# A hybrid layer (state scan, latent attention, expert mixer): the order of TensorE's front, rewritten

## The chip, the cores and the metric
One core of a Trainium2 chip runs the whole layer in one program. The metric is the device time of one execution in microseconds. The five engines are TensorE (PE), VectorE (DVE), ScalarE (ACT), GpSimd (POOL) and SyncE (SP, which only issues DMAs here).

## The reference, cut to what matters
Two groups of 128 tokens, a prompt (g = 0) and a sample (g = 1), go through the same layer of width 1024, all in float32.

```python
def trunk_layer(x, cvec, p, rope=None, ctx=None):
    sh1, sc1, g1, sh2, sc2, g2 = modulation(cvec, p['w_mod'], p['b_mod'])   # 1024 -> 6 x 1024
    h = modulate(x, p['norm1'], sh1, sc1)                                   # rmsnorm * (1 + scale) + shift
    u, c_q, c_kv, k_rope = jnp.split(h @ p['w_in'], IN_SPLITS, axis=-1)
    ssm_out, ssm_state = s5_mixer(u, p, ...)      # diagonal state scan, both directions, gated
    ...                                           # latent attention, 8 heads; the sample also reads 128 cached tokens
    mix = jnp.concatenate([ssm_out, attn], axis=-1) @ p['w_out']
    x = x + g1 * mix
    h2 = modulate(x, p['norm2'], sh2, sc2)
    x = x + g2 * peer(h2, p['w_query'], p['sub_keys'], p['u_table'], p['v_table'])
```

`peer` makes 8 heads of two queries from h2 and scores them against 128 keys each. It takes the 16 best of each, then the 16 best sums, so 128 experts ("picks") per token. It reads a row of u and a row of v for each, and adds gelu(h2 . u) * gate * v. Both groups together take 256 picks for each of 128 partitions. One pick is a gather of 128 rows of 2048 floats (u and v side by side), 1 MB.

## The kernel before
**Stages.** TensorE's order is written out by hand (lines 757 to 897). First come eight steps of the first modulation quarter (`quad_step(0, k)`) and the transposes of the normed inputs; then the S5 scan in four chunks of units u = 0 to 3. Each chunk has `input_weights`, `input_projection`, `input_chunked` and `s5_in` on TensorE; `s5_products`, `s5_scans` and `s5_turns` on DVE; `s5_sums`, `s5_turns` and `s5_last` on POOL; and then `y_local`, `y_carried` and `y_spread` on TensorE again. Between these stand the projections to the latents of both groups, their transposes, the attention of the prompt, and the steps of the second modulation quarter. Then come the gate, the output product of the prompt (`out_projection`), the second norm (`norm2_of`, on rows), its transposes, the queries and scores, and the sample's attention up to its scores.

**The carried state.** `y_carried(u)` (line 582) multiplies four parts of the turned state for each of eight tiles and halves: 64 products, in pairs with the same weights. Chunk 3 uses chunk 0's work area again, so its sums wait for `y_ready` and `last_ready`.

**The loop of picks.** It has 64 iterations `it` of four picks. POOL gathers a pick (line 1316) into one of the memory pages of 8 KB per partition that are in turn. `row_plan` (line 68) fixes which: four at the start (13, 14, 8, 9), 15 from pick 4, 0 and 1 from picks 5 and 6, then 6 and 7 from 24, 3 and 4 from 88. A page is used again when its last pick is accumulated (`row_free`), and a new one when `available` says so. DVE takes the dot product with h2 (line 1626). ACT makes gelu and weight and writes them as a diagonal matrix (`weigh`, line 1061): it waits for all four dots of the iteration, then four small weights, then four diagonals. TensorE adds diagonal times v (`accumulate`, line 746), eight products of 512 columns, and frees the page. In the first 26 iterations TensorE does other work ahead of each accumulation (lines 849 to 896): at `it` 0 the rest of the sample's attention and its whole output product, then rows of the norm, and whole sets of queries and scores. DVE finds the picks of a unit of 32 (`find`, `number`, `normalise`) between its dots; the first unit is split by heads, and the gathers start when `number(0, (0, 1))` is done.

**What sets the order.** Each engine runs its list in order and waits on semaphores. A PSUM bank is given by `bank_plan` (line 84): each name has a bank and a turn, and TensorE's `start` waits until the turn before is emptied. SP loads weights in the order of `PAGES` (line 55) and waits, in that order, until a page's last user is done.

## Time and profile before
| | us |
|---|---|
| median of 3 runs | 973.76 (971.82 to 975.36) |
| profiled execution, its own time | 973.73 |
| its span, first to last instruction | 971.9 |
| TensorE busy in it | 771.5 (79%) |
| DVE busy | 555.8 (57%) |
| POOL busy | 350.2 (36%) |
| ACT busy | 253.8 (26%) |
| bytes moved | 324.21 MB, mean 334 GB/s |

The busy shares are means over stages that have different limits. The view of slices and the view of stretches show how a stage runs; the view in order of time shows who starts when, and the idle time in brackets behind a row is that of the engine just before it, with what ended it. One call of a 512-column product appears as two instructions, so eight products are "x16".

### The profile page before, as it was taken

Reading aid. Unit: us, or ns where it says so; the run is one execution under the profiler, and the core shown is the slowest. Engines: PE = TensorE matmul, PEld = TensorE weight load, DVE = VectorE, ACT = ScalarE, POOL = GpSimd, SP = SyncE. Lnnn points to the kernel's source line nnn. Section 1 sums busy time; section 2 is a strip of 40 time slices with the busy share of each in tenths; the row PEclk is TensorE's granted clock in tenths of the full one; section 3 lists DMA queues with packets and bytes.
Section 4 is the critical chain, followed back from the end, with each engine's and each line's share of the span. In section 5 each row is a group of like instructions: output and inputs, shape, how many; then the busy total and the mean of one; then the engine's idle time right before and its main releaser. Section 6 shows DMA issues by size and latency. Waiting matters only on the chain. (4 is left out here: it accounts for less than half of the span.)

```text
span 971.9 us, 11540 instructions
## 1 busy us (share of the span) xinstructions
PE 771.5 (79%) x4265; PEld 409.0 (42%) x4265; DVE 555.8 (57%) x1211; ACT 253.8 (26%) x804; POOL 350.2 (36%) x326
## 2 busy tenths in 40 slices
PE   3898979884878799989979887886975868677785
PEld 0586655544535355646523333332332323233332
DVE  7923261135742863684476559549847845954543
ACT  3411342123321232232222132213211312222120
POOL 1511341001113434324434543543753544264430
PEclk9899999998789999999989998988999898899898
DMA  9840571722466999999999999999999999999991
GB/s 371 322 162 3 223 321 71 277 98 78 161 259 232 363 420 420 420 395 383 384 421 422 421 419 422 420 420 422 419 420 421 392 423 421 371 417 422 422 421 61
DMA packets 46383, 324.21 MB, mean 334 GB/s; under 512 B 5420, under 2 KB 5996, under 8 KB 8184
## 3 DMA queue, kind: packets, MB, share of 16 engines
q0 software_dynamic: 36864, 268.45, 67.6%
q1 hardware_dynamic: 9096, 54.86, 14.2%
q8 instruction: 33, 0.54, 0.2%
q10 hardware_dynamic: 368, 0.18, 0.1%
q14 instruction: 22, 0.18, 0.0%
HBM read 322.24 MB, written 1.23 MB: 333 GB/s over the span
## 5 line engine op out<-in xcount | busy, mean ns | idle before, releaser
L746 PE MATMUL psum<-mem 128*128 128x512 f32 x1024 | 484.1, 630 | 125.0 <-ACT mem L1077 121.5
L1316 POOL DMA_INDIRECT mem<-uv_table,small x256 | 299.1, 1168 | 434.3 <-PE psum L746 350.5
L1626 DVE CUSTOM_DVE_ANT_0 mem<-mem,h 128x1024 f32<-128x1024 f32 x256 | 309.5, 1227 | 250.9 <-DMA mem<-uv_table,small 248.8
L746 PEld LDWEIGHTS psum<-mem 128*128 128x128 f32 x1024 | 201.7, 202 | 397.7 <-issue 243.7
L1065 ACT ACTIVATE small<-small 128x4 f32<-128x4 f32 x64 | 13.2, 206 | 487.3 <-DVE small L1626 487.3
L1077 ACT ACTIVATE mem<-consts,small 128x128 f32<-128x128 f32 x256 | 80.8, 387 | 0.0
L725 PE MATMUL psum<-hT,mem 128*128 128x128 f32 x512 | 60.2, 280 | 4.8 <-DVE mem L1521 3.3
L725 PEld LDWEIGHTS psum<-hT,mem 128*128 128x128 f32 x512 | 59.9, 196 | 8.6 <-issue 7.0
L1070 ACT ACTIVATE small<-small 128x1 f32<-128x1 f32 x256 | 54.5, 283 | 5.9
L1245 POOL TENSOR_SCALAR small<-small 128x1 f32<-128x1 f32 (+1 forms) x9 | 2.8, 309 | 120.7 <-DVE small L1526 41.7
L462 PE MATMUL psum<-mem,scol 128*32 128x512 f32 x128 | 21.5, 766 | 16.9 <-DMA mem<-w_mod 16.4
L1462 DVE TENSOR_TENSOR mem<-psum,mem 128x512 f32<-128x512 f32 x16 | 9.9, 684 | 42.2 <-PE psum L566 42.2
L1487 DVE SCALAR_TENSOR_TENSOR yb<-h,consts,psum 128x256 f32<-128x256 f32 x4 | 1.9, 481 | 48.1 <-PE psum L602 48.1
L910 ACT COPY late<-psum 128x512 f32<-128x512 f32 (+2 forms) x36 | 19.8, 580 | 35.1 <-PE psum L734 9.6
L707 PE MATMUL psum<-mem,hT 128*128 128x512 f32 x64 | 28.0, 593 | 0.0
L486 PE MATMUL psum<-modrow,consts 128*128 128x512 f32 (+1 forms) x32 | 18.1, 695 | 5.7 <-DVE mem L1512 5.7
L1582 DVE FIND_INDEX8 mem<-mem 128x8 uint32<-128x128 f32 (+1 forms) x64 | 21.8, 352 | 0.0
L1285 POOL TENSOR_TENSOR mem<-mem 128x528 f32<-128x528 f32 x8 | 11.0, 1384 | 29.7 <-DVE mem L1479 28.6
L1626 DVE DVE_READ_ACCUMULATOR2_ANT small<- 128x1 f32 x256 | 21.1, 82 | 0.0
L1579 DVE MAX8 mem<-mem 128x8 f32<-128x128 f32 (+1 forms) x64 | 19.4, 350 | 0.9
L1579 DVE MAX8 mem<-late 128x8 f32<-128x128 f32 x32 | 7.1, 281 | 20.3 <-ACTq L1054 20.3
L707 PEld LDWEIGHTS psum<-mem,hT 128*128 128x128 f32 x64 | 12.1, 190 | 14.8 <-issue 14.8
(193 smaller groups left out, 648.0 us busy)
## 6 DMA issues: line engine op xcount, KB each, us to landing
mem<-w_mod SPq DMA_DIRECT2D x24, 1024.0 KB, 10.4
mem<-w_query SPq DMA_DIRECT2D x8, 1024.0 KB, 9.2
mem<-w_out SPq DMA_DIRECT2D x4, 1024.0 KB, 12.4
mem<-uv_table,small POOLq DMA_INDIRECT x256, 14.6
mem<-w_uq SPq DMA_DIRECT2D x4, 576.0 KB, 5.2
mem<-w_in_u SPq DMA_DIRECT2D x2, 1024.0 KB, 15.6
mem<-w_ukv SPq DMA_DIRECT2D x2, 1024.0 KB, 5.3
mem<-w_in_qkv SPq DMA_DIRECT2D x2, 1008.0 KB, 10.0
```

What stands on the lines that cost most here:

```text
L462: mm = pe.matmul(out[32 * j:32 * j + 32, :], scol[:, k, :], w[:, j, :], start=k == 0, stop=False, tile_position=(0, 32 * j))
L486: mm = pe.matmul(out, ident[lo:hi, j + g:j + g + 1].to_broadcast([hi - lo, P]), modrow[lo:hi, n // 4, :], start=True, stop=True, tile_posi ...
L707: mm = pe.matmul(out, mixT[:, k, P * g:P * g + P], weight(f"out{half}.{k // 4}", 512, 4)[:, k % 4, :], start=first and i == 0, stop=last a ...
L725: mm = pe.matmul(out[:, P * i:P * i + P], weight(m, 512, 4)[:, k % 4, P * i:P * i + P], hT[:, k, P * g:P * g + P], start=k == 0, stop=k == ...
L746: mm = pe.matmul(bank(f"acc_{g}_{half}"), diag[:, pick % DEEP, :], row_of(pick)[:, D + 512 * half:D + 512 * half + 512], start=first and k ...
L910: empties(act.copy(dst, src), name)
L1070: act.activation(wts[:, slot:slot + 1], gel[:, slot:slot + 1], ACT.Copy, scale=gate[:, pick:pick + 1]).then_inc(wts_ready, 1)
L1077: act.activation(diag[:, slot, :], ident, ACT.Copy, scale=wts[:, slot:slot + 1]).then_inc(diag_ready, 1)
L1316: pool.indirect_dma_start(row_of(pick), None, uv_table, bass.IndirectOffsetOnAxis(ap=idx[:, pick:pick + 1], axis=0)).then_inc(row_landed[R ...
L1579: last = dve.max(out_v[:, r, first_:first_ + 8], row)
L1582: last = dve.max_index(out_i[:, r, first_:first_ + 8], out_v[:, r, first_:first_ + 8], row)
L1626: dve.tensor_tensor_reduce(out=row[:, 0:D], in0=row[:, 0:D], in1=h[:, it // NB, :], scale=1.0, scalar=0.0, op0=ALU.mult, op1=ALU.add, accu ...
```

## The change
- TensorE's front has a new order. All four `s5_in` come before the latents. Two steps of modulation quarter 1 at a time are put between the chunks. The sample's query and key projections (`attention_queries(1)`, `attention_keys(1)`) stand behind the prompt's output product, between the first queries and scores. Their weights stay in their pages from the prompt's use, so that three loads (uq2.0, uq2.1, ukv2) are gone.
- Each chunk has its own work area. POOL adds the two parts of the turned state (`sum_ready`), and `y_carried` has half the products.
- The biases of a modulation quarter are added after step 5 and not after step 7. x is loaded after two weight steps and cmat later.
- The second norm for the queries is no longer made on rows and transposed. TensorE multiplies x with a diagonal of the root (`normed_turned`), which transposes and scales at once; scale and shift are columns (`columns_turned`, `norm_columns`), applied in the eviction. The row form of h2, which the dots need, is still made, for the sample only at `it` 22 and 23.
- Queries and scores of the first unit are split in halves (`first_queries`, `first_scores`); the other queries are made in two iterations each. Half of the sample's output product comes before its attention scores, the other half at `it` 4 and 5.
- `weigh` goes pick by pick.
- The pages in turn are other ones and open at other times (`row_plan`, `available`).

```diff
-SCORED = [0, 1, 4, 5, 2, 6, 3, 7]
+SCORED = [0, 0, 1, 2, 4, 5, 3, 6, 7]
+FOUND = [2, 4, 6, 7, 8, 9, 10, 11]
...
-    free, arriving = [13, 14, 8, 9], {4: 15, 5: 0, 6: 1, 24: 6, 25: 7, 88: 3, 89: 4}
+    free, arriving = [6, 7, 8, 9], {4: 4, 5: 13, 16: 15, 64: 0, 65: 1, 96: 2, 97: 3, 120: 5}
...
-            for k in range(4):
+            for k in range(2):
                 load(f"mod0.{k}")
             sp.dma_start(x[:, 0, :], x_prompt).then_inc(x_in, 16)
             sp.dma_start(x[:, 1, :], x_sample).then_inc(x_in, 16)
...
             def y_carried(u):
-                pe.wait_ge(qd_ready, 2 * u + 2)
-                pe.wait_ge(qp_ready, 2 * u + 2)
+                pe.wait_ge(sum_ready, 2 * u + 2)
...
-                        for k, (r, b) in enumerate(((0, 0), (0, 2), (1, 1), (1, 3))):
+                        for r in range(2):
...
+            def normed_turned(g):
+                pe.wait_ge(rootd_ready, g + 1)
                 for q in range(2):
+                    out = start(f"h2T_{g}_{q}")
+                    for i in range(4):
+                        k = 4 * q + i
+                        mm = pe.matmul(out[:, P * i:P * i + P], x[:, g, P * k:P * k + P], root_diag[g], start=True, stop=True)
+                    finish(mm, f"h2T_{g}_{q}")
...
             pe.wait_ge(ssm_ready, 1)
             for half in range(2):
                 out_projection(0, half, range(4), last=True)
+            columns_turned()
...
-            attention_queries(1)
-            attention_keys(1)
-            h2_transposed(0)
-            queries(0, 0)
-            scores(0, 0)
+            attention_queries(1, (0,))
+            normed_turned(0)
+            attention_queries(1, (1,))
+            first_queries(0)
+            attention_keys(1, 0, "k")
+            first_scores(0)
+            first_queries(1)
+            attention_keys(1, 0, "v")
+            first_scores(1)
+            attention_keys(1, 1)
             heads_turned(1)
+            pe.wait_ge(ssm_ready, 2)
+            for half in range(2):
+                out_projection(1, half, range(4), first=True)
             attention_scores(1)
 
             for it in range(NU):
-                if it == 0:
+                if it in (0, 1):
+                    queries(0, 1, it)
+                elif it == 2:
+                    scores(0, 1)
                     probs_turned(1)
+                elif it == 3:
                     attended(1)
                     spread_row("g1", 1)
+                elif it in (4, 5):
                     wait_emptied(pe, "at1")
-                    pe.wait_ge(ssm_ready, 2)
-                    for half in range(2):
-                        out_projection(1, half, range(8), first=True, last=True)
+                    out_projection(1, it - 4, range(4, 8), last=True)
...
             def weigh(it):
...
+                for pick in range(BATCH * it, BATCH * it + BATCH):
+                    slot = pick % DEEP
+                    cut_ = slice(slot, slot + 1)
+                    act.wait_ge(dots_ready, pick + 1)
+                    act.activation(gel[:, cut_], dots[:, cut_], ACT.Gelu_apprx_tanh).then_inc(gel_ready, 1)
+                    act.wait_ge(gates_ready, it + 1)
+                    act.wait_ge(gel_ready, pick + 1)
+                    act.activation(wts[:, cut_], gel[:, cut_], ACT.Copy, scale=gate[:, pick:pick + 1]).then_inc(wts_ready, 1)
                     act.wait_ge(wts_ready, pick + 1)
                     if pick >= DEEP:
                         act.wait_ge(row_free, pick - DEEP + 1)
+                    act.activation(diag[:, slot, :], ident, ACT.Copy, scale=wts[:, cut_]).then_inc(diag_ready, 1)
...
+                for r in range(2):
+                    pool.wait_ge(qp_ready, 2 * u + 2)
+                    pool.tensor_tensor(view(u, r), view(u, r), view(u, 2 + r), ALU.add).then_inc(sum_ready, 1)
...
             def available(page_):
-                if page_ in (13, 14):
-                    pool.wait_ge(y_ready, NC)
-                    pool.wait_ge(last_ready, 2 * NC)
+                if page_ == 6:
+                    wait_filled(pool, "q_1_1")
+                elif page_ == 7:
+                    wait_filled(pool, "v2")
                 elif page_ in (8, 9):
                     pool.wait_ge(h2_ready, 1)
+                elif page_ == 4:
+                    pool.wait_ge(out_used, 1)
+                elif page_ == 13:
+                    pool.wait_ge(out_used, 2)
                 elif page_ == 15:
                     wait_filled(pool, "at1")
                 elif page_ in (0, 1):
-                    wait_filled(pool, f"mix_1_0")
+                    wait_filled(pool, "qry_1_1")
...
             for u in range(NC):
-                if u == 0:
-                    inverse_root(rstd_a[:, 0:2], ms_a[:, 0:2], [(0, 1, QR), (1, 2, KVR)], sqa_ready, 2, rstda_ready)
                 if u + 1 < NC:
                     s5_sums(u + 1)
...
+                if u == 3:
+                    inverse_root(rstd_a[:, 0:2], ms_a[:, 0:2], [(0, 1, QR), (1, 2, KVR)], sqa_ready, 2, rstda_ready)
                 s5_turns(u)
```

The new front on TensorE, from the first `s5_in` on: s5_in(0); chunk and projection pairs; s5_in(1); two steps of quarter 1; s5_in(2); kernels; s5_in(3); latents(0); steps 2, 3; toeplitz; latents_turned(0); y(0); steps 4, 5; latents(1); the prompt's queries and keys; y(1); steps 6, 7; latents_turned(1); heads_turned(0); y(2); attention_scores(0); y(3) carried; two steps of quarter 2; y_spread(3); probs_turned(0); g1 row; attended(0); the gate products between the halves of the output product; two steps of quarter 2; the rest of the output product; columns_turned; rows for the norm.

## Rows read from the trace of the kernel before
**Rows 1.** The page's 40 slices: GB/s that the DMA engines moved in each.
```profile
GB/s 371 322 162 3 223 321 71 277 98 78 161 259 232 363 420 420 420 395 383 384 421 422 421 419 422 420 420 422 419 420 421 392 423 421 371 417 422 422 421 61
```

**Rows 2.** DMA queues: packets, MB, share of 16 engines; the gathers' queue.
```profile
q0 software_dynamic: 36864, 268.45, 67.6%
```

**Rows 3.** TensorE in order of time: start, us, line, operation, count, [idle before].
```profile
40.89 7.14 PE L512 MATMUL psum<-hT,mem 128*128 128x256 f32 x32 [1.93 <-ACT hT L922]
...
115.58 3.90 PE L592 MATMUL psum<-mem 64*64 64x64 f32 x128
...
205.89 7.10 PE L644 MATMUL psum<-mem,yb 128*128 128x512 f32 x16 [2.65 <-DVE h L1536]
212.83 1.04 PE L493 MATMUL psum<-consts,h 128*128 128x128 f32 x8
215.30 7.38 PE L725 MATMUL psum<-hT,mem 128*128 128x128 f32 x64 [1.43 <-ACT hT L910]
223.41 1.16 PE L734 MATMUL psum<-mem,yb 128*128 128x128 f32 x8 [0.73 <-ACT yb L910]
...
228.57 3.69 PE L668 MATMUL psum<-late 96*128 96x256 f32 x16 [1.37 <-ACT late L910]
245.88 3.67 PE L493 MATMUL psum<-consts,mem 128*128 128x128 f32 x16 [13.62 <-DVE mem L1680]
...
256.46 13.90 PE L707 MATMUL psum<-mem,hT 128*128 128x512 f32 x32
270.19 7.03 PE L746 MATMUL psum<-mem 128*128 128x512 f32 x16
...
954.34 8.83 PE L746 MATMUL psum<-mem 128*128 128x512 f32 x16 [2.78 <-ACT mem L1077]
```

**Rows 4.** Stretches: busy us of PE, PEld, DVE, ACT, POOL; clock, DMA, GB/s.
```profile
236.00:340.00 104.00, 78.52 (x267) 43.91 (x268) 58.20 (x155) 25.27 (x77) 29.02 (x31) 0.84 0.68 255
340.00:480.00 140.00, 130.74 (x609) 83.58 (x608) 81.45 (x180) 38.88 (x126) 53.02 (x48) 0.99 0.99 403
...
560.00:946.00 386.00, 294.20 (x616) 122.74 (x617) 252.82 (x573) 98.73 (x362) 181.66 (x151) 0.92 1.01 416
```

**Rows 5.** GpSimd in order of time: first, eighth and thirty-first gather.
```profile
235.47 1.22 POOL L1316 DMA_INDIRECT mem<-uv_table,small  x1 [32.47 <-DVEq L1609]
...
272.35 0.94 POOL L1316 DMA_INDIRECT mem<-uv_table,small  x1 [6.40 <-PE psum L746]
...
349.36 0.94 POOL L1316 DMA_INDIRECT mem<-uv_table,small  x1 [0.78 <-PE psum L746]
```

**Rows 6.** DVE in order of time: first find, first numbers, first and last product.
```profile
225.34 0.49 DVE L1579 MAX8 mem<-late 128x8 f32<-128x128 f32 x2 [17.45 <-ACTq L1054]
...
234.93 0.17 DVE L1607 SCALAR_TENSOR_TENSOR small<-mem 128x16 uint32<-128x16 f32 x1
...
245.74 1.22 DVE L1626 CUSTOM_DVE_ANT_0 mem<-mem,h 128x1024 f32<-128x1024 f32 x1
...
951.58 1.23 DVE L1626 CUSTOM_DVE_ANT_0 mem<-mem,h 128x1024 f32<-128x1024 f32 x1 [1.22 <-DMA mem<-uv_table,small]
```

**Rows 7.** TensorE's waits from 139 to 225 us: in total, times, longest.
```profile
PE psum L493 <- issue: 5.6, 1, 5.6
...
PE psum L697 <- ACT yb L1153: 2.3, 1, 2.3
...
PE psum L474 <- DMA mem<-w_mod: 1.4, 1, 1.4
...
PE psum L602 <- ACT h L1034: 0.5, 1, 0.5
```

**Rows 8.** Line 1285, POOL's products of the scan: ns minimum, median, maximum.
```profile
L1285 POOL TENSOR_TENSOR mem<-mem x8: 1213/1282/2164, 105.3 to 158.7; 128x528 f32<-128x528 f32 x8
```

**Rows 9.** Line 1316, the gathers: from issue to landing.
```profile
DMA to landing us min/median/max: 5.6/14.6/18.3
```

**Rows 10.** Line 746, one instruction of the accumulation: ns minimum, median, maximum.
```profile
L746 PE MATMUL psum<-mem x1024: 592/592/1222, 270.2 to 962.6; 128*128 128x512 f32 x171
```

More of the change, by code:

```diff
@@ new lines, in bank_plan @@
+    four, six = [2, 3, 6, 7], [4, 5, 0, 1, 2, 3]
+    order += [(n, four[i % 4]) for i, n in enumerate(("q_1_0", "h2T_0_0", "h2T_0_1", "q_1_1", "qry_0_0a", "k1", "sc_0_0a", "qry_0_0b"))]
+    names = ["v1", "sc_0_0b", "k2", "v2",
+             "qT_1_0", "qT_1_1", "kT_1_0", "kT_1_1", "kT_2_0", "kT_2_1"]
+    order += [(n, six[i % 6]) for i, n in enumerate(names)]
+    order += [("mix_1_0", 6), ("mix_1_1", 7)]
+    order += [(f"s_1_{q}", 2 + q) for q in range(4)]
+    four, wide = [2, 3, 4, 5], [2, 3, 4, 5, 6, 7]
@@ L389, in _ @@
             sp.dma_start(x[:, 1, :], x_sample).then_inc(x_in, 16)
-            for k in range(4, 6):
+            for k in range(2, 6):
                 load(f"mod0.{k}")
@@ L445, in arrived, with bias @@
                 pe.wait_ge(landed[at_], 16 * sum(where == at_ for _, where in PAGES[:ORDER[name] + 1]))
-            def bias(q, js):
+            def bias(q, js, last=True):
                 if q == 0:
@@ L461, in quad_step @@
                 for j in range(4):
-                    mm = pe.matmul(out[32 * j:32 * j + 32, :], scol[:, k, :], w[:, j, :], start=k == 0, stop=False, tile_position=(0, 32 * j))
-                mm.then_inc(mod_used, 1)
-                if k == KD - 1:
-                    finish(bias(q, range(4)), name)
+                    mm = pe.matmul(out[32 * j:32 * j + 32, :], scol[:, k, :], w[:, j, :], start=k == 0, stop=k == KD - 1,
+                                   tile_position=(0, 32 * j))
+                if k < KD - 1:
+                    mm.then_inc(mod_used, 1)
+                else:
+                    finish(mm, name)
+                    wait_filled(pe, name)
+                    pe.sem_inc(mod_used, 1)
+                if k == KD - 3:
+                    bias(q, range(4), last=False)
             def pair_step(s, i):
@@ L633, in attention_queries, with attention_keys @@
                     finish(mm, f"q_{g}_{q}")
-            def attention_keys(g):
+            def attention_keys(g, b, kinds="kv"):
                 wait_emptied(pe, f"ckvT_{g}")
-                name = f"ukv{'2' if g else ''}"
-                arrived(name)
-                w = weight(name, 512, 4)
-                for b in range(att[g].blocks):
-                    for m, kind in enumerate("kv"):
+                arrived("ukv")
+                w = weight("ukv", 512, 4)
+                for m, kind in enumerate("kv"):
+                    if kind in kinds:
                         out = start(f"{kind}{att[g].b0 + b}")
@@ L833, in _ @@
+            pair_step("a", 2)
+            pair_step("a", 3)
+            pe.wait_ge(ssm_ready, 1)
+            for half in range(2):
+                out_projection(0, half, range(4), last=True)
+            columns_turned()
             pe.wait_ge(y_read, NC)
```

609 lines of the change are left out of this document (331 added, 278 removed), and 2 rows, old and new, of the table LAST_USE.

## The prediction
> **What bounds the kernel now.** I read the slices of the page first, then the DMA queues, the stretches by stage, the waits and the instructions in order of time. The slices show two halves of a different kind [rows 1]: up to a third of the span the bytes per second jump between 3 and 371 GB/s, and from there to the end they stand at 420 with few dips. Nearly all of the bytes of the second half are expert rows: the gathers' queue moved 268.45 MB [rows 2], so 256 gathers of 1.05 MB, and at 420 GB/s one takes 2.5 us and an iteration of four takes 10.0 us. An iteration's eight products take 7.03 us on TensorE [rows 3], less than those 10. The stretch 560 to 946 runs at 416 GB/s with TensorE busy for 294 of 386 us: DMA is the bound. 340 to 480 runs at 403 GB/s with TensorE busy for 131 of 140 us: the queries and scores between the picks make the two nearly equal. 236 to 340 runs at 255 GB/s [rows 4]. So the end is set by three times: when the first gather goes, how long it then takes until DMA is full, and the tail behind the last gather.
>
> The first gather goes at 235.5 [rows 5]; it waits for the numbers of the first head, which end at 235.1 and begin at 225.3 with a wait of 17.5 us for the first scores [rows 6]. Those leave TensorE at 223.41 + 1.16 = 224.6 [rows 3]. Ahead of that TensorE is full but for eight waits, 15.7 us in all between 139 and 225 [rows 7]. Four gathers then go at once. The first row is freed by the first accumulation, which starts at 270.2, since TensorE first has the sample's probabilities, attended values and 13.9 us of output product before it. The eighth gather goes at 272.4, the thirty-first (pick 30) at 349.4 [rows 3, 5]. From there on DMA is full, and every microsecond won or lost before pick 30 arrives at the end unchanged. I follow that one gather.
>
> **The change, up to the first scores** (before: 224.6).
> (a) The inputs x are ahead of two weight steps in SP's queue, the bias of the first modulation no longer ends it, and the angles' second half comes behind hT on DVE. TensorE waits 1.9 us for hT before its first input projection [rows 3]. Between 0 and -4; I take -2, that wait.
> (b) The sums of the carried state are made on POOL, so each of four carried products has half its instructions: 4 x 3.90 / 2 = -7.8. The price is two more adds per chunk on POOL. An operation of that size took 1.21 to 2.16 us there [rows 8]; POOL's chain of the four chunks then ends near 98 us (four times two multiplications and two adds, 5 us at the median, behind the last inputs of the scan, which now reach DVE at about 78), and up to 14 us later at the maximum; the last carried product stands at about 133 in TensorE's order. Hidden. What is not covered is the root of the prompt's latents, which has moved behind three chunks on POOL and is needed by TensorE at about 96: it is ready near 94 at the median and up to 6 us late at the maximum. I take 0, keep +6.
> The row behind (b) has a median near its minimum and one far end. The Trainium skill (SBUF — State Buffer, SBUF: two separate sides) says that VectorE and GpSimd share a port pair as an exclusive lock, so that the loser blocks for a whole instruction. It speaks against giving POOL more work beside DVE's scans; if every added operation met it, the root would be the 6 us late, and the time 924 and not 918. The maximum agrees with the rule, the median says that it is met seldom.
> (c) Behind the first scores now: three of the four key and value products of the sample (7.10 x 3/4 = -5.3), half of the first queries (7.38 / 2 = -3.7) and half of the scores (-0.6): -9.6 [rows 3]. The find of the first head needs only that half.
> (d) The waits. The 15.7 us go: the 5.6 in which TensorE stands ahead of the prompt's probabilities, because two chunks of y and two modulation steps are put there; the 2.7 for banks, which are planned anew; the 1.4 for a weight and the 2.3 for the gelu in the main [rows 7]. New ones, each counted from the operations that ScalarE and DVE have in line: spreading chunk 3 waits for exp and scaling of the probabilities (about 2.3), the gate product for the gate row's eviction and the gelu (1.8), the norm's product for square sum, root and diagonal (0.5), a weight step and two pipeline drains (0.7): 5.3. Net -10.4. Were they twice as long, -5; none, -15.7.
> (e) The norm's columns add about 1.0 and the product with the diagonal of the root 0.8 over the transpose (twice the instructions on 1.04 us); 1 us is given back where products run slow behind the 5.6 us wait (the same instruction takes 592 to 1222 ns, [rows 10]). +0.8.
> Sum -2 - 7.8 - 9.6 - 10.4 + 0.8 = -29.0, bounds -20 and -36. First scores end at 195.6, first gather at 206.5.
> SP drops three loads (2.2 MB), which lay where DMA was idle: 0. The second output weights wait for the last chunk of y, about 135, and land by 151; they are used at about 158: 0.
>
> **The change, from the first scores to pick 30.** Between 195.6 and the sample's attention scores TensorE has the other half of queries, scores and keys (3.7 + 0.6 + 5.3), the head transposes (2.8) with about 1.3 of waiting for the key's rope, half of the sample's output product (13.9 / 2 = 7.0) and the scores (3.7): they end at 220. The products' start before lies 13.5 behind that end (232.3 to 245.7, [rows 3, 6]), of which 5 were DVE's find and maxima, done by then now: 228.6, that is -17. Pages 4 and 13 are freed by the half output product at about 212 to 216, so six rows are under way instead of four.
> Now the larger part. The first accumulation no longer has the 24 us from 245.9 to 270.2 ahead of it, and a pick is weighed as soon as its own dot is there: 228.6 + 1.2 + 1.1 = 230.9, against 270.2: -39. The starts of the next ones by TensorE's order: it 1 at 243.5 (8.8 as in the last accumulation of [rows 3], since TensorE has stood idle before, and half a query 3.7); it 2 at 257.4 (7.0, scores 1.1, transposes 1.9, and 4 of waiting for the bank of the second scores, which ScalarE empties only behind its own weights of that iteration); it 3 at 270.6 (7.0, attended and gate row, 6.2 of the 6.9 us between the transposes and the output product in [rows 3]); it 4 at 281.1, it 5 at 291.6 (7.0 and a quarter of 13.9 each). Pick 30 needs the last row of it 5 with seven pages in turn: 298.7, against 349.4: **-51**. With the bounds above, and 3 either way for these steps, -42 to -61.
>
> **From pick 30 to the end.** 226 gathers and the same weights are left, DMA-bound before and after. Two things differ. Before, nine pages were in turn from pick 25 on; now seven until pick 63, nine until 95, then eleven and twelve, and picks 16, 64, 96 and 120 wait for the page they open. Loop of a page: issue 1.2, landing at least 5.6 [rows 9], dot 1.2, weight 1.1, product 1.8, together 11 us against 17.5 us that seven rows take at full rate; 6.5 us of it may be blocked, and half a find with its number takes DVE 9.8 us in two pieces (225.3 to 235.1, [rows 6]). So a few bubbles: +4, up to +24. The other: queries are cut in halves over 2 to 24, so TensorE has 7.0 and at most half of 7.38 in one iteration instead of all of it; before, 340 to 480 lost (421 - 403) / 421 x 140 = 6 us. I take -2 of it. Together **+2**.
> Tail: the last dot ends at 952.8 and the last accumulation 10.4 us later (1.5 for the weights of four, then 8.83) [rows 3, 6]. With picks one by one only the last one is left: 1.1 (of the 1.5, three small weights go) and 1.8 to 2.4. **-6.5** (-3 to -7). Four times 1.1 us of ScalarE per iteration fit into 10.
>
> **Sum.** The profiled run took 973.73 (span 971.9 and 1.8 around it), the median of the runs is 973.76: no correction. 973.7 - 51 + 2 - 6.5 = **918**.
>
> **Rivals.**
> *Seven pages starve the loop.* Picks 16 to 63 in twelve iterations with half a find or a number on DVE in five of them, and half a query on TensorE in most: where the blocks add instead of overlapping, an iteration takes 2 us more. For it: the ramp of before had seven pages and made 255 GB/s. Against: it had TensorE blocks of 9 to 24 us, now at most 6. 973.7 - 51 + 26 - 6.5 = 942.
> *The ramp keeps its length.* Pick 16 waits for the attended values and holds POOL's queue behind it; if that and the second scores' bank come late, the 104 us from the first product to pick 30 stay: -17 and not -51: 952. Against: 39 us of it is TensorE's order, which the diff changes.
> *Slower: TensorE's clock falls under the loop.* Picks come one by one, 1.8 us of product and a pause. An accumulation takes 7.03 us and the last one, behind a pause, 8.83; one instruction took 592 ns and up to 1222 [rows 3, 10]. At the lower level (1.2 GHz) an iteration takes 14.1 us, over the 10.0 of DMA; from a mean granted clock under 0.70 TensorE is the bound. To eat the 56 us in the 56 iterations from pick 30 on takes 11 us each, a mean of 0.64; all at 0.5 it is +230. For it: 0.84 granted in the ramp [rows 4]. Against: 0.92 from 560 to 946, where TensorE is idle for a quarter of the time, and the new pauses are shorter.
> The Trainium skill (TensorE: Matmul & The Clock Gate, The HAM clock gate) says that the array is throttled by default and that activity releases it. It would make this rival's time 975 or more if short bursts did not count as activity; the 0.92 beside a quarter of idle time agrees with the rule and speaks for the full level.
>
> **How the numbers follow.** Forecast (903 to 933) 0.72; better than that (banks and waits all hidden, first scores at 189) 0.05; starving 0.14; ramp unchanged 0.05; clock 0.04. The range 898 to 943 leaves out the last two and a little of each end. A measurement of this kernel tells 0.3% from no change. Faster 0.95, same 0.01, slower 0.04.
>
> **What would show it.** First gather at 206 (200 to 216), first accumulation at 231, pick 30 at 299 (290 to 309), no long waits of TensorE between 80 and 200 but for about 2 us near 140; carried products at 2 us; 420 GB/s from 300 on, with dips near picks 64 and 96; 4 us from the last dot to the last product's end. Wrong would be: iterations 4 to 15 longer than 11 us, a granted clock under 0.8 there, or TensorE waiting for POOL's sums.

## The result, and the profile after

The changed kernel took **924.63 us** (median of 4 runs, 921.98 to 926.78), the kernel before 974.46 us beside it (4 runs, 971.82 to 975.36): ratio 0.949, 95% interval 0.946 to 0.953. Forecast were 918 us, range 898 to 943. The profiled run has a span of 920.2 us (before: 971.9), so 51.7 us went. The time is 6.6 us above the forecast.

TensorE in order of time, kernel after (start, us, line, operation, count, [idle before]), against [rows 3]:

```profile
39.19 7.14 PE L522 MATMUL psum<-hT,mem 128*128 128x256 f32 x32 [2.04 <-ACT hT L978]
...
100.53 2.19 PE L532 MATMUL psum<-h,consts 128*32 128x64 f32 x73 [3.17 <-issue]
...
127.97 2.03 PE L601 MATMUL psum<-mem 64*64 64x64 f32 x64
...
148.74 0.65 PE L611 MATMUL psum<-h,consts 128*32 128x64 f32 x32 [2.04 <-ACT h L1085]
...
155.04 3.84 PE L705 MATMUL psum<-yb,mem 128*128 128x128 f32 x32 [1.88 <-ACT yb L1224]
...
188.44 2.05 PE L737 MATMUL psum<-mem,x 128*128 128x128 f32 x16 [1.08 <-ACT mem L1096]
...
197.56 0.61 PE L769 MATMUL psum<-mem,yb 128*128 128x128 f32 x4
...
217.28 3.62 PE L676 MATMUL psum<-late 96*128 96x256 f32 x16
...
233.09 8.51 PE L789 MATMUL psum<-mem 128*128 128x512 f32 x16 [6.07 <-ACT mem L1143]
241.44 3.73 PE L745 MATMUL psum<-hT,mem 128*128 128x128 f32 x32
245.01 7.03 PE L789 MATMUL psum<-mem 128*128 128x512 f32 x16
...
260.29 1.12 PE L503 MATMUL psum<-consts,mem 128*128 128x128 f32 x4 [6.04 <-ACT late L966]
261.19 8.05 PE L789 MATMUL psum<-mem 128*128 128x512 f32 x16
...
909.39 1.98 PE L789 MATMUL psum<-mem 128*128 128x512 f32 x4 [0.48 <-ACT mem L1143]
```

The reader is to see three things. The first-half scores (L769) end at 198.2, where the full ones ended at 224.6. The first accumulation (L789) starts at 233.1 and has the loop's other work behind it, not ahead of it; before it started at 270.2. And the last accumulation is no block of 16 behind a wait any more, but a piece of 4.

The gathers, kernel after, against [rows 5] (first, eighth, pick 30, pick 96):

```profile
208.83 1.21 POOL L1406 DMA_INDIRECT mem<-uv_table,small  x1 [20.87 <-DVEq L1721]
...
238.44 0.94 POOL L1406 DMA_INDIRECT mem<-uv_table,small  x1 [0.78 <-PE psum L789]
...
303.57 1.25 POOL L1406 DMA_INDIRECT mem<-uv_table,small  x1 [1.23 <-PE psum L789]
...
493.19 1.57 POOL L1406 DMA_INDIRECT mem<-uv_table,small  x1 [15.29 <-PE psum L745]
```

Two pages freed by the half output product let the fifth and sixth gather go at 214.8 and 217.7; the seventh waits for the first accumulation. The stretches, kernel after, with the columns of [rows 4]:

```profile
236.00:340.00 104.00, 89.37 (x315) 47.02 (x315) 70.91 (x174) 43.52 (x127) 38.13 (x39) 0.93 0.92 365
...
340.00:480.00 140.00, 132.73 (x545) 78.14 (x544) 94.28 (x235) 56.92 (x172) 61.50 (x53) 0.98 1.01 420
460.00:500.00 40.00, 39.19 (x140) 21.78 (x140) 27.49 (x50) 17.93 (x52) 12.91 (x12) 0.94 0.90 364
560.00:900.00 340.00, 272.62 (x564) 104.12 (x564) 223.15 (x491) 137.86 (x431) 159.76 (x134) 0.94 1.01 421
```

The ramp moves 365 GB/s where it moved 255, and from 300 on the queue is full but for one hole, near 480 us, where POOL stands 15.3 us before pick 96. The last dot and the end, kernel after, against [rows 6]:

```profile
907.05 1.23 DVE L1738 CUSTOM_DVE_ANT_0 mem<-mem,h 128x1024 f32<-128x1024 f32 x1 [1.23 <-DMA mem<-uv_table,small]
...
910.63 0.69 DVE L1747 TENSOR_TENSOR late<-psum,late 128x512 f32<-128x512 f32 x1 [2.35 <-PE psum L789]
```

From the start of the last dot to the end of the span it is 13.1 us (before: 971.9 - 951.6 = 20.3). So the books are: up to pick 30, 303.6 - 349.4 = -45.8; from there to the last dot, (907.05 - 303.57) - (951.58 - 349.36) = +1.3; tail -7.2. The sum is -51.7, the whole difference of the spans.

### The profile page after: what moved, and what is told of

It is laid out like the page before. It is cut to its first block and busy times, and to the rows that moved or that the text cites. A ratio compares the mean times of both kernels' runs of the same rounds, so it can differ in the third digit from the quotient of the medians.

```text
span 920.2 us, 11502 instructions
## 1 busy us (share of the span) xinstructions
PE 761.9 (83%) x4033; PEld 388.1 (42%) x4033; DVE 562.1 (61%) x1225; ACT 341.9 (37%) x1008; POOL 354.8 (39%) x334
## 5 line engine op out<-in xcount | busy, mean ns | idle before, releaser
L789 PE MATMUL psum<-mem 128*128 128x512 f32 x1024 | 488.8, 623 | 109.2 <-ACT mem L1143 108.2
L1406 POOL DMA_INDIRECT mem<-uv_table,small x256 | 291.5, 1139 | 396.0 <-PE psum L789 309.3
L789 PEld LDWEIGHTS psum<-mem 128*128 128x128 f32 x1024 | 191.7, 197 | 392.5 <-issue 198.6
L1136 ACT ACTIVATE small<-small 128x1 f32<-128x1 f32 x256 | 51.9, 203 | 374.8 <-DVE small L1738 366.2
L1143 ACT ACTIVATE mem<-consts,small 128x128 f32<-128x128 f32 x256 | 102.9, 402 | 8.4
L1139 ACT ACTIVATE small<-small 128x1 f32<-128x1 f32 x256 | 75.4, 295 | 24.8 <-ACT small L1136 1.1
L966 ACT COPY late<-psum 128x512 f32<-128x512 f32 (+3 forms) x37 | 19.4, 570 | 6.2 <-PE psum L652 2.4
L966 ACT COPY mem<-psum 128x512 f32<-128x512 f32 (+2 forms) x20 | 10.6, 539 | 29.2 <-PE psum L532 16.2
L522 PE MATMUL psum<-hT,mem 128*128 128x256 f32 x64 | 14.6, 383 | 2.0 <-ACT hT L978 2.0
L532 PE MATMUL psum<-h,consts 128*32 128x64 f32 x512 | 13.2, 271 | 3.2 <-issue 3.2
## 6 DMA issues: line engine op xcount, KB each, us to landing
mem<-uv_table,small POOLq DMA_INDIRECT x256, 23.5
```

The lines of the kernel that those rows point to most:

```text
L789: mm = pe.matmul(bank(f"acc_{g}_{half}"), diag[:, pick % DEEP, :], row_of(pick)[:, D + 512 * half:D + 512 * half + 512], start=first and k ...
L966: empties(act.copy(dst, src), name)
L1136: act.activation(gel[:, cut_], dots[:, cut_], ACT.Gelu_apprx_tanh).then_inc(gel_ready, 1)
L1139: act.activation(wts[:, cut_], gel[:, cut_], ACT.Copy, scale=gate[:, pick:pick + 1]).then_inc(wts_ready, 1)
L1143: act.activation(diag[:, slot, :], ident, ACT.Copy, scale=wts[:, cut_]).then_inc(diag_ready, 1)
L1406: pool.indirect_dma_start(row_of(pick), None, uv_table, bass.IndirectOffsetOnAxis(ap=idx[:, pick:pick + 1], axis=0)).then_inc(row_landed[R ...
```

## The experiments

Eleven kernels. They were run in three batches, each with the kernel before beside it, to which the ratios are taken: the first four here, with before at 974.28 us (median); then four with one edit each (seven pages in either kernel, the evictions, pages 2 and 3), at 975.93; then the three that join edits, at 974.46. "Before" and "after" name the two kernels of the case. A difference in us is taken to the 974.46 or the 924.63 of the result, unless it says otherwise.

**Weights of picks four at a time, in the kernel after.** My theory, T1, was: TensorE's new order up to pick 30 carries nearly all, and the weights only the tail.

```diff
-                for pick in range(BATCH * it, BATCH * it + BATCH):
-                    act.wait_ge(dots_ready, pick + 1)
+                act.wait_ge(dots_ready, BATCH * (it + 1))   # gelu of four, then four weights, then four diagonals
```

> The kernel after, with the weights of picks made four at a time again (ScalarE waits for all four dots of an iteration, as in the kernel before). Theory 1 (weights one by one give the tail and shorten the way from a landed row to a freed page): the tail, from the start of the last dot to the end of the span, goes from 13.2 us back to 20 (+7); the first accumulation starts after the fourth dot, +2 to +3; with seven pages in turn a page's loop is about 4 us longer, so iterations 1 to 15 lose 5 to 10 us together: 924.6 + 7 + 8 = 940 (934 to 948). Rival 2 (only the tail, since DMA is full either way from the thirty-first gather on): 932.

Measured: 963.88 us (961.29 to 964.56), ratio to before 0.987 (0.984 to 0.991). Both numbers were far too low: the weights are worth 39 us in the new kernel. The first gather still goes at 209.2, but pick 30 goes at 322.3, pick 64 at 430.2 and pick 128 at 611.7, where the kernel before had it at 615.7. All of the 26 us of lead but 4 has gone by then. Its stretches, to be held against the 420 GB/s of after:

```profile
340.00:460.00 120.00, 106.61 (x427) 63.20 (x425) 64.77 (x147) 30.57 (x107) 45.02 (x41) 0.92 0.93 363
```

TensorE is idle for 13 of the 120 us and DMA isn't full: neither is the bound by itself, so pages come back too late. The tail went back only to 18.7 us, not to 20.3: the last accumulation took 7.13 us here and 8.83 in before.

**Weights one by one, in the kernel before** (the same edit the other way round, nothing else).

> The kernel before, with only the weights made one by one. Theory 1: the tail gives 7 us; the ramp gives little, because its first accumulation stands behind 24 us of other work on TensorE and nine pages are in turn from pick 25 on (-1 to -4): 974.5 - 10 = 965 (961 to 968). Rival 3 (most of the gain of the whole change is the shorter loop of a page, not TensorE's order): 950 or less.

Measured: 955.51 us (952.43 to 964.24), ratio 0.980 (0.973 to 0.987): -19 (-13 to -26 by the interval), between the two theories. In its profile the tail is 13.0 us, 7.3 less; the rest has come in by pick 64 (443.8, against 452.4).

**Sums of the carried state taken back from POOL, in the kernel after.**

```diff
-                        for r in range(2):
+                        for k, (r, b) in enumerate(((0, 0), (0, 2), (1, 1), (1, 3))):
-                for r in range(2):
-                    pool.wait_ge(qp_ready, 2 * u + 2)
-                    pool.tensor_tensor(view(u, r), view(u, r), view(u, 2 + r), ALU.add).then_inc(sum_ready, 1)
```

> The kernel after, with the carried state again in four parts: POOL makes no sums, each carried product has 128 instructions and takes 3.9 us and not 2.0. Theory 1 (TensorE's order up to the first accumulation is the path, each microsecond on it arrives at the end): four times 1.9 us, of which the last one is in part covered by the 2.0 us for which TensorE waits ahead of spreading chunk 3: first accumulation at 239 and not 233, time 930.5 (929 to 933). Rival 4 (the two sums on POOL delay TensorE about as much as they save, through the port pair that DVE and POOL share): 924 to 926.

Measured: 930.77 us (927.69 to 932.42), ratio 0.954 (0.950 to 0.958): 6.1 us more than after, as T1 said. Its first gather goes at 215.2 and pick 30 at 310.1, 6.4 and 6.5 us late, so the shift of TensorE's front arrives at the end one to one. TensorE in this kernel (three of the four carried products), against 2.03 us each in after:

```profile
104.47 4.56 PE L602 MATMUL psum<-mem 64*64 64x64 f32 x128
129.52 3.90 PE L602 MATMUL psum<-mem 64*64 64x64 f32 x128
...
147.54 3.90 PE L602 MATMUL psum<-mem 64*64 64x64 f32 x128
```

The POOL sums cost nothing that can be seen here, though POOL's root of the prompt's latents is ready at 97.1 without them and at 101.4 with them: at that place TensorE stops in both kernels (3.46 and 3.17 us, with nothing to wait for), and the stop hides it.

**All keys and values of the sample ahead of its first queries, in the kernel after.** This puts three of the four key and value products back to where they were, 5.3 of the 9.6 us of step (c), on TensorE and in ScalarE's evictions.

```diff
+            attention_keys(1, 0)
+            attention_keys(1, 1)
             first_queries(0)
-            attention_keys(1, 0, "k")
             first_scores(0)
             first_queries(1)
-            attention_keys(1, 0, "v")
             first_scores(1)
-            attention_keys(1, 1)
```

> The kernel after, with all four key and value products of the sample ahead of the first queries, as in the kernel before; the same work up to the sample's attention scores, in another order. The first gather goes 5.4 us later (214 and not 209). Theory 1 (what counts is when the first rows are freed, that is the first accumulation, which waits for the sample's attention and not for the first rows): first accumulation at 233 as now, time 924 to 926. Rival 5 (an earlier first gather arrives at the end): 930.

Measured: 924.15 us (923.42 to 930.28), ratio 0.949 (0.945 to 0.954). The first gather goes at 213.9, 5.1 us later than in after, and the time is the same. The four rows that go then are not used until the first accumulation, which TensorE reaches behind the same sum of work either way (here 0.8 us later, with 1.6 us less of waiting):

```profile
213.91 1.21 POOL L1404 DMA_INDIRECT mem<-uv_table,small  x1 [26.75 <-DVEq L1719]
```

```profile
233.86 9.28 PE L789 MATMUL psum<-mem 128*128 128x512 f32 x16 [4.44 <-ACT mem L1142]
```

So these 5 us of an earlier first gather were worth nothing by themselves. That leaves the 39 and the 19 us of the weights to be explained. The theory that I formed from the first kernel's profile, S: a page given back in fours stays out longer than seven pages can cover.

**Seven pages up to pick 64, in the kernel before.**

```diff
-    free, arriving = [13, 14, 8, 9], {4: 15, 5: 0, 6: 1, 24: 6, 25: 7, 88: 3, 89: 4}
+    free, arriving = [13, 14, 8, 9], {4: 15, 5: 0, 6: 1, 64: 6, 65: 7, 88: 3, 89: 4}
```

> The kernel before with one edit in its page plan: its pages 6 and 7 join at picks 64 and 65, not 24 and 25, so the gathers run with seven pages up to pick 64 as they do in the changed kernel; the weights stay four at a time. Theory S (what the changed order with weights four at a time loses after its early first gather is starvation: seven pages are too few when a page is given back in fours): the 420 GB/s of 340 to 452 us fall to what that run had there (329, 367 and 392 GB/s in three stretches), which is 8.7 + 5.0 + 2.1 = 16 us: 990 us (range 982 to 998), with DVE's dots not waiting for the queue but POOL waiting for TensorE. Rival R (pages are enough; that run lost its lead because its TensorE order leaves queries and output products between the accumulations): 974 to 978 us.

Measured: 997.68 us (992.06 to 999.08), ratio 1.021 (1.012 to 1.029): +22 to the kernel before beside it. That is in the range of S (982 to 998) and far from the rival. Up to pick 20 its profile goes with that of before (323.0 and 322.8); at pick 64 it is 26.6 us behind. Its stretch:

```profile
340.00:460.00 120.00, 101.72 (x453) 64.32 (x453) 64.74 (x153) 29.72 (x95) 34.59 (x33) 0.91 0.89 345
```

**Both: seven pages up to pick 64 and weights one by one, in the kernel before** (the two edits shown above).

> The kernel before with two edits: seven pages up to pick 64 (its pages 6 and 7 join at 64 and 65), and weights one by one. Theory S (starvation comes of pages and fours together; one by one, seven pages are enough): no more than the nine-page kernel with weights one by one had (955.5 us): 957 us (954 to 961), with 420 GB/s between 340 and 460 us. Rival (seven pages cost the old TensorE order its 22 us whatever the weights do, since its queue was never as deep as the new kernel's): 970 us or more.

Measured: 959.25 us (956.76 to 960.61), ratio 0.983 (0.977 to 0.989). S had said 957 us (954 to 961), the rival 970 or more. With weights one by one the two pages are worth 3.7 us, within the spread of the runs; with weights by fours they are worth 22. Its stretch and its first waits in it (in total, times, longest), then those of the kernel with fours:

```profile
340.00:460.00 120.00, 114.05 (x531) 72.59 (x530) 73.56 (x166) 49.89 (x148) 45.27 (x45) 1.00 1.01 413
```

```profile
DVE mem L1622 <- DMA mem<-uv_table,small: 43.2, 28, 6.2
...
PE psum L746 <- ACT mem L1073: 5.9, 2, 3.0
```

```profile
POOL mem L1316 <- PE psum L746: 82.2, 30, 11.9
DVE mem L1626 <- DMA mem<-uv_table,small: 49.8, 20, 8.5
...
PE psum L746 <- ACT mem L1077: 18.3, 5, 5.2
```

With fours POOL waits 82.2 us for accumulations to free a page while DMA isn't full (share 0.89; one by one it waits as long, 82.4 us, but with rows enough under way that the share is 1.01); DVE waits for 20 rows, up to 8.5 us for one, and TensorE stands 18.3 us for weights. The rows come late because their pages were given back late. S holds, and the stops cost more than their own length: behind each of the five TensorE takes 8.6 to 10.0 us for an accumulation of 7.03, 9.9 us more in all. Behind the first (idle until 359.0) the granted clock is 0.50 from 359 to 363 us, so the lower level (1.2 GHz), and 1.00 again from 365. One by one the waits in this stretch are two, of up to 3.0 us, the mean clock is 1.00, and the accumulations take 7.0 to 7.3 us. The clock is thus a part of what fours and seven pages cost together; no run separates it.

**Seven pages up to pick 93, in the kernel after** (pages 0 and 1 join at 94 and 95 instead of 64 and 65).

> The changed kernel with its pages 0 and 1 joining at picks 94 and 95, not 64 and 65: seven pages for thirty picks more, weights one by one. Theory S (one by one, a page comes back 1 to 2 us after its own dot, so seven pages hold the queue full, as the 419 and 421 GB/s of 340 to 420 us show): 924 to 927 us. Rival (seven pages only just do beside sparse work on TensorE, and starve once the second block's queries lie between the accumulations): 930 us or more, GB/s below 400 between 400 and 490 us.

Measured: 924.51 us (923.82 to 925.78), ratio 0.947 (0.940 to 0.954), the time of after. Seven pages are enough for it through the second block's queries too:

```profile
400.00:460.00 60.00, 59.90 (x252) 35.49 (x250) 35.41 (x92) 22.57 (x73) 26.87 (x24) 1.00 1.01 421
```

**Second block's scores and probabilities evicted ahead of the weights of picks 8 to 11.** The wait of 6.04 us at 260.3 in the profile after.

```diff
             for it in range(NU):
+                if it == 2:
+                    scored(0, 1)
                 weigh(it)
...
                 elif it == 2:
-                    scored(0, 1)
                     attention_evac(1)
```

> The changed kernel with one stretch of ACT's order turned round: the evictions of the second block's scores and probabilities go ahead of the weights of picks 8 to 11, so that TensorE's transposes of the probabilities don't wait 6.04 us (from 254.2 to 260.3) behind those weights. Theory T1 (the time is set by TensorE's order up to pick 30): third accumulation at about 256 instead of 261.2, pick 30 at 299 instead of 303.6, the whole 919.5 us (917 to 922). Rival (landing of the first gathers and DVE's top-k set the ramp just behind it): the 6 us turn up as waits for weights at the next accumulations, 923 to 925 us.

Measured: 919.01 us (916.15 to 922.96), ratio 0.943 (0.936 to 0.950): -5.6. In its profile the transposes follow without the stop and the third accumulation starts 6.7 us earlier, at 254.5. 1.7 of these are not the edit's, since its first gather already goes 1.7 us earlier (207.1), where the two kernels are the same:

```profile
251.20 1.91 PE L503 MATMUL psum<-consts,mem 128*128 128x128 f32 x16
254.46 7.13 PE L789 MATMUL psum<-mem 128*128 128x512 f32 x16 [1.35 <-ACT mem L1143]
```

**Pages 2 and 3 join at picks 104 and 105 instead of 96 and 97.**

> The changed kernel with its pages 2 and 3 joining at picks 104 and 105, not 96 and 97. At pick 96 POOL stands 15.3 us in its order until TensorE's last queries of the second block (L745) have ended, and GB/s fall from 420 to 306 between 480 and 500 us. Theory T1 (behind pick 30 the time is the queue's bytes, and a hole in it is never made good): the hole is 5.4 us of queue time at 420 GB/s between 460 and 500 us, so 919.5 us (917 to 922). Rival (the hole moves with the page plan, since TensorE's queries come later as well when accumulations have more to do): 923 to 926 us.

Measured: 920.12 us (919.13 to 921.49), ratio 0.942 (0.936 to 0.949): -4.5. The hole is gone:

```profile
460.00:500.00 40.00, 35.75 (x127) 19.70 (x127) 30.29 (x59) 18.13 (x53) 14.71 (x13) 0.91 1.01 421
```

**Both edits.**

> The changed kernel with both edits that each gave time alone: evictions of the second block's scores and probabilities ahead of the weights of picks 8 to 11 (-5.6 us alone), and pages 2 and 3 joining at picks 104 and 105 (-4.5 us alone). Theory T1 (each removes its own hole in the queue, one at 254 us and one at 480 us): the two add, and the second hole was a little deeper with the first edit (341 instead of 364 GB/s in 460 to 500 us), so 913.5 us (911 to 916). Rival (the holes trade places, as the second grew when the first went): 917 to 920 us.

Measured: 912.62 us (910.64 to 914.49, 6 runs), ratio 0.935 (0.931 to 0.940), 12.0 below after, for 10.1 of the two alone. They add.

**Both edits, and the dots of picks 0 to 3 ahead of the second block's softmax sum.** In after DVE takes the dots of the first four rows at 229.3 without waiting for one of them, and TensorE stands 6.07 us before the first accumulation.

```diff
 ACT
-            attention_exp(1)
             soft_exp(1, 0, TOPK)
+            attention_exp(1)
 DVE
             softmax_max(1)
             normalise(0, 0, (0, 1))
+            products(0)
             softmax_sum(1)
...
             for it in range(NU):
-                products(it)
-                if it == 0:
+                if it:
+                    products(it)
+                else:
```

> The kernel with both edits, and a third: DVE's dots of picks 0 to 3 go ahead of the sum of the second block's softmax and the multiplication of its probabilities (2.29 us), and ACT's exponential of the gates ahead of that block's, so that the first weights leave ACT at about 226.5 us, not 231.2. Theory T1: TensorE's first accumulation follows its queries without the wait of 3.16 us, and of that the next two keep 1 to 3: 911.5 us, 2 below the kernel with both edits (range 3 to 0 below). Rival (the landing of gathers 8 to 11 sets the third accumulation, so nothing is left of it): the same time as the kernel with both edits, within 1 us.

Measured: **906.39 us** (905.57 to 911.11, 6 runs), ratio 0.929 (0.925 to 0.934), 6.2 below the kernel with both edits, three times what I gave it and outside the range of 3 to 0; it beats both kernels of the case, after by 18 us. The direction was right and the size wrong. I took the 3.16 us of the kernel with the eviction alone for the wait, but a wait is only what is left behind the work ahead of it: there the queries ran at a granted clock of 0.50 (222 to 226 us) and took 6.72 us, with both edits 3.81, and in both kernels the first accumulation starts at 231.4. The kernel with both edits shows a wait of 6.08 at that place, and this one 1.40:

```profile
231.40 10.05 PE L789 MATMUL psum<-mem 128*128 128x512 f32 x16 [6.08 <-ACT mem L1143]
```

```profile
228.34 7.11 PE L789 MATMUL psum<-mem 128*128 128x512 f32 x16 [1.40 <-ACT mem L1143]
```

It starts 3.1 us earlier, though the first gather goes 1.6 us later in this profile (208.7 for 207.1). The block is 2.9 us shorter as well (7.11 for 10.05), and that is the clock: with both edits the granted clock is 0.50 from 231 to 237 us, behind the wait, and here it stays at 1.00. The two together are the 6.0 us by which the second accumulation (244.9 to 238.9) comes earlier, and with it the ninth gather (240.6 to 234.5) and pick 30 (297.4 to 291.4). ScalarE's table load of 1.28 us ahead of the first gelu has left the path, too: it stood behind the first dot (228.94), and here it ends before (225.88 to 227.16).

The landmarks of the profiles side by side, in us (start of a gather; the tail is from the last dot's start to the end of the span):

| kernel | first gather | pick 30 | pick 64 | pick 128 | tail | median |
|---|---|---|---|---|---|---|
| before | 235.5 | 349.4 | 452.4 | 615.7 | 20.3 | 974.5 |
| before, one by one | 238.8 | 346.9 | 443.8 | 606.6 | 13.0 | 955.5 |
| before, seven pages | 235.8 | 354.7 | 479.0 | 639.7 | 20.3 | 997.7 |
| before, seven pages, one by one | 235.1 | 345.7 | 443.5 | 603.4 | 13.0 | 959.3 |
| after, by fours | 209.2 | 322.3 | 430.2 | 611.7 | 18.7 | 963.9 |
| after | 208.8 | 303.6 | 399.7 | 572.9 | 13.1 | 924.6 |
| after, three edits | 208.7 | 291.4 | 387.4 | 556.0 | 13.2 | 906.4 |

The table's first six rows give the parts of the change, as medians from different batches; worked out from the ratios, the differences are the same to within 4 us. At seven pages the new order is worth 997.7 - 963.9 = 33.8 us with fours and 959.3 - 924.6 = 34.7 one by one. At seven pages one by one is worth 38.4 in the old order and 39.3 in the new one. The page plan costs 23.2 with fours (997.7 - 974.5; 21.8 to the kernel before beside it) and 3.7 one by one. So in the whole time order and weights add within the spread of the runs; weights and pages don't. "Order" here is everything in the diff but the weights and the seven pages: of its 34 us the sums on POOL are 6, the later keys and values 0, and the rest was not taken apart.

## Why the prediction came out

**The bound, right.** The time came out 6.6 us above the forecast and within its range. Full queue from 300 on, so pick 30 carries the shift: -45.8 there and -51.7 at the end. In the kernels without the sums, with the eviction and with the early dots, what a stop of TensorE took or gave at pick 30 is the difference of the medians to within 2.2 us, about as much as one profile differs from another of the same front (first gathers at 207.1 to 209.2). It has one limit, which the prediction's wording missed: *before* the first accumulation a microsecond of the first gather is worth nothing. Five were given back for 0.

**Steps (a) to (e), first scores, -29 forecast, -26.4 measured** (197.56 + 0.61 against 224.6).

- (a) 39.19 for 40.89: -1.7, not by losing the wait (2.04 us are still there), but because what stands ahead of it comes earlier.
- (b) 2.67 and three times 2.03 us for 3.90, 3.90, 4.79 and 3.90: -7.7, and undone it costs 6.1; POOL's root is ready at 101.4, not 94: the chain as I added it up left out what POOL also does for each chunk (the sums ahead of the scan, 2.5 to 3.5 us, and small copies), and one pair of sums took 3.87 us, not twice 1.31. Nothing waited for it, but that was luck. TensorE stopped for 3.17 us just ahead of the transposes that need it; without the stop it would have stood there at about 99.5 (102.65 - 3.17) and waited some 3 us (an estimate), half of the 6 that I kept for it.
- (c) happened as forecast, but 5.3 of its 9.6 us are the keys and values, and those are worth nothing.
- (d) The three new waits were forecast at 2.3, 1.8 and 0.5 and measured 2.04, 1.88 and 1.08. Added up over all of TensorE's waits behind the start of its first input projection up to the first scores it is 13.5 us, for 22.3 in before: -8.8, where -10.4 was forecast. What was not seen is a wait of 1.72 us for a modulation weight at 68.4, and that the stops inside runs of small products come to the same sum (6.4 and 6.2 us) though fewer of these products are left, one of them 3.17 us.

Some 0.6 us of the step's miss is not assigned.

**From the first scores to the first accumulation.** The first product at 229.3 (forecast 228.6), the first accumulation at 233.1 (230.9), the second at 245.0 (243.5), the third at 261.2 (257.4), since the bank of the second scores cost 6.04 us and not 4; the fourth at 272.9 (270.6), the fifth at 283.2 (281.1), the sixth at 295.4 (291.6); pick 30 at 303.6 (298.7). The misses against the forecast times are four. The first accumulation is 2.2 late, of which 1.28 are ScalarE's table load ahead of the first gelu, which had no term. The slow products behind that wait were forecast (8.8 us, measured 8.51); the granted clock is 0.50 from 231 to 235 us. The bank took 2 us more, and 1.5 came back behind it. A wait of 1.74 us for the weights of the sixth accumulation had no term, and the last row came 1.1 later than a block of 7.0 puts it. Together, less what came back, they are the 5 us of the term -51.

**What the term -51 was made of, left open by the forecast.** The prediction gave the weights one by one 6.5 us of tail and no price of their own in the ramp. At pick 30 the two can't be parted by one number, because each is worth more beside the other. With seven pages pick 30 goes at 354.7 (old order, fours), 345.7 (old order, one by one), 322.3 (new order, fours) and 303.6 (both): the weights are worth 9 us in the old order and 19 in the new one, the order 32 with fours and 42 one by one. From the kernel before, whose pages 6 and 7 join at pick 24, the order alone gives 27.1 of the 45.8 us and the weights alone 2.5. The order is the larger part whichever way it is counted. The 39 us that TensorE no longer has ahead of its first accumulation were true (37.1 measured); I followed them through a loop in which a row was weighed as soon as its dot was there, and so the term was about right for both edits together and says nothing of either alone.

**The loop, +2 forecast, +1.3 measured; its reason was half wrong.** I asked whether seven pages starve and counted a page's loop at 11 us against the 17.5 that seven rows take. That count holds one by one. By fours the first row of a batch waits for three more (3 x 2.5 us), which makes it 1.2 + 5.6 + 1.2 + 7.5 + 1.5 + 1.8 = 18.8 us (an estimate from rows of before): over 17.5, but under the 22.5 of nine pages. The estimate tells which side of the limit a kernel is on, and not how much it loses: 18.8 over 17.5 would be 7% of the rate, and the two kernels lost 14 and 18% of 421 GB/s. Blocks of other work ahead of an accumulation and the lower clock behind a wait come on top. The prediction's rival "seven pages starve the loop" (942) is what happened in both kernels with fours and seven pages (363 and 345 GB/s); against it I named TensorE's smaller blocks, where what spoke against it was the weights. The blocks didn't decide: the old order one by one has whole queries of 7.31 us between its accumulations from 340 to 460 us and keeps 413 GB/s there with seven pages.

The bubbles of the real loop were one: 15.3 us of POOL before pick 96, for which TensorE's last queries of the second block had to end. The prediction said "dips near picks 64 and 96"; there was none at 64, and the one at 96 cost 4.5 us.

**The tail, -6.5 forecast, -7.2 measured.** One piece of 1.98 us, 0.48 behind its diagonal, for 8.83 us behind 2.78. Of the 8.83 us 1.8 are the clock's: before shows a granted clock of 0.50 from 955 to 957 us.

**The rivals.** *The ramp keeps its length*: no; it is 74.2 us from the first product to pick 30 (229.3 to 303.6), for 103.6. *TensorE's clock*: the granted clock is 0.94 from 560 to 900, so near the upper level (2.4 GHz), with pauses behind every piece; before it was 0.92. The mean over the span was higher in the profile of every kernel with weights one by one (0.948 to 0.962) than in those with fours (0.916 to 0.933), so the rival had the sign wrong. *The port pair* (the Trainium skill, SBUF — State Buffer, SBUF: two separate sides, says that VectorE and GpSimd block each other on it for whole instructions): of POOL's eight added sums the minimum is 1.30, the median 1.31 and the maximum 2.15 us; three of the four pairs took 2.57 to 2.61 us and the one at 95.5 took 3.87. The trace fits the rule in that one pair, though it doesn't name the cause; no time hung on it.

## What to carry to other kernels

Where a loop gathers rows into few pages, add up one page's way (issue, landing, wait for the rest of its batch, weight, product) and hold it against pages times transfer time: how finely the consumer gives pages back can be worth as many microseconds as the number of pages, and each makes the other cheap. Here one edit of ScalarE's order was worth 19 us with nine pages and 38 with seven. A transfer that starts earlier was worth nothing here until the step that frees its buffer started earlier too; look for the engine that does that step, and for small work (a multiplication, four evictions) that stands ahead of it in an order written by hand. A wait in a profile is what is left behind the work ahead of it: before pricing its removal, look at whether that work ran at the full clock. When a forecast bundles two edits in one landmark, work the landmark out once with each alone: the sum can be right with its parts unknown.

## What the runs showed of the hardware

- A gather's median time from issue to landing went up from 14.6 us [rows 9] to 23.5 us while the kernel became 5% faster. The queue is deeper, and each row still takes 2.5 us of it (1.05 MB at 420 GB/s). That number measures the depth, not a cost:

```profile
DMA to landing us min/median/max: 6.2/23.5/26.9
```

- TensorE stops for 0.8 to 3.2 us inside long runs of 64-column products, with nothing that the profile shows to wait for: 0.79, 1.48, 0.99 and 3.17 us in after between 75 and 101 us, 1.73, 1.50, 1.21 and 1.74 us in before between 69 and 93 us. What it is stays open; no experiment here aimed at it.
- The first accumulation behind a wait of 6.1 us took 8.51 and 10.05 us in two kernels, 9.28 behind 4.4 us, 8.62 behind 3.2 us and 7.11 behind 1.4 us, where the stream takes 7.03. The granted clock tells it: 0.50 from 231 to 235 us in after and from 231 to 237 with both edits, and 1.00 throughout with the three edits. In after TensorE had ended its queries at 227.0; the granted clock is 1.00 until 229 and 0.50 from 230 on. In the four kernels with waits of 3.2 us and more the wait cost a quarter to half of its length again in the products behind it.
